# Differential attention: the pooling branch's GpSimd operations, each as two operations of half the columns

## The reference

```python
def diff_attention(q, k, v, lam, g_sub, lam_init):
    def one(qblk):
        s = jnp.einsum('bqhsd,bkhsd->bhsqk', qblk, k).astype(jnp.float32) * scale
        p = jax.nn.softmax(s, axis=-1)
        a = p[:, :, 0] - lam * p[:, :, 1]
        return jnp.einsum('bhqk,bkhe->bqhe', a.astype(v.dtype), v)
...
def multiscale_pool(u, w_pool, pool_scale):   # POOL_WINDOWS = (2, 4, 8, 16), one per 128 channels
...
    w = jnp.array(POOL_WINDOWS, dtype=jnp.int32)
    lo = jnp.clip(t - w // 2, 0, n)
    hi = jnp.clip(t + w - w // 2, 0, n)
    wsum = csum[:, hi, grp] - csum[:, lo, grp]
    pooled = (wsum / count - uf).astype(u.dtype)
    y = jnp.einsum('bngc,gcd->bngd', pooled, w_pool).reshape(b, n, BRANCH_WIDTH)
    return y * pool_scale
```

## Time and profile before

| what | value |
|---|---|
| median of 3 runs | 1798.11 us (1797.95 to 1799.56) |
| the profiled execution's own time | 1797.41 us |
| its span, first to last instruction | 1795.6 us |
| TensorE busy | 1742.4 us (97%) |
| VectorE busy | 1228.7 us (68%) |
| ScalarE busy | 805.7 us (45%) |
| GpSimd busy | 755.7 us (42%), 464 instructions |
| mean granted TensorE clock | 0.997 of full speed |

### The profile page before, as it was taken

The page is one execution under the profiler, slowest core; times in us unless marked ns, Lnnn a source line. Parts: engine busy times, 40 slices in busy tenths (PEclk is TensorE's granted clock), DMA queues, the critical chain, the costliest instruction groups (busy, mean ns, idle before and its releaser), DMA issues. The chain is left out here.

```text
span 1795.6 us, 25730 instructions
## 1 busy us (share of the span) xinstructions
PE 1742.4 (97%) x9180; PEld 1482.6 (83%) x9180; DVE 1228.7 (68%) x1719; ACT 805.7 (45%) x1580; POOL 755.7 (42%) x464
## 2 busy tenths in 40 slices
PE   8999999999998999999999999999999999999998
PEld 6997888888877899888888878778888888888886
DVE  3528688879948999677743366876556556476767
ACT  3435343434637788655530045733333333344453
POOL 0307678776534877520022241455555555400000
PEclk9999999999999999999999999999999999999999
DMA  8333233435777566412024332223323323386734
GB/s 312 118 101 125 111 117 153 162 132 188 258 194 181 137 164 180 115 32 71 1 103 154 131 141 95 94 94 105 117 93 105 130 103 106 126 273 203 257 107 176
DMA packets 98376, 249.86 MB, mean 139 GB/s; under 512 B 12258, under 2 KB 25954, under 8 KB 98147
## 3 DMA queue, kind: packets, MB, share of 16 engines
q1 hardware_dynamic: 98274, 248.52, 41.6%
HBM read 183.07 MB, written 65.41 MB: 138 GB/s over the span
## 5 line engine op out<-in xcount | busy, mean ns | idle before, releaser
L729 POOL TENSOR_TENSOR ring<-raw_w,ring 128x512 fp32r<-128x512 f32 x120 | 187.0, 1576 | 138.7 <-ACT ring L600 138.6
L78 PE MATMUL psum<-h_hi,ring 128*128 128x512 f32 x400 | 156.5, 391 | 2.6 <-ACT z L646 2.0
L79 PE MATMUL psum<-h_lo,ring 128*128 128x512 f32 x400 | 156.3, 391 | 0.0
L80 PE MATMUL psum<-h_hi,ring 128*128 128x512 f32 x400 | 156.1, 390 | 0.0
L78 PE MATMUL psum<-u_slot 128*128 128x512 f32 x308 | 120.4, 391 | 1.0 <-DVE u_slot L2898 0.9
L80 PE MATMUL psum<-u_slot 128*128 128x512 f32 x308 | 120.1, 390 | 0.0
L79 PE MATMUL psum<-u_slot 128*128 128x512 f32 x308 | 119.9, 389 | 0.0
L600 ACT ACTIVATE ring<-raw_w 128x512 fp32r<-128x512 f32 x120 | 72.6, 625 | 100.0 <-DVE raw_w L889 32.8
L1353 DVE TENSOR_REDUCE mx<-psum 128x1 f32<-128x1280 f32 x64 | 95.1, 1487 | 7.0 <-PE psum L1239 6.2
L1286 ACT ACTIVATE e<-psum,neg_m 128x1280 f32<-128x1280 f32 x64 | 85.0, 1329 | 31.6 <-DVE neg_m L1354 31.6
L2497 POOL TENSOR_TENSOR cut_lo<-i_raw,cut_hi 128x512 fp32r<-128x512 f32 x44 | 66.9, 1520 | 59.2 <-ACT cut_hi L2352 59.2
(11 more groups left out here) (409 smaller groups left out, 5222.2 us busy)
## 6 DMA issues: line engine op xcount, KB each, us to landing
raw_w<-in_w_pairs SPq DMA_DIRECT2D x40, 512.0 KB, 4.6
qk_dram<-room SPq DMA_DIRECT2D x26, 512.0 KB, 3.6
room<-in_w_ada SPq DMA_DIRECT2D x24, 512.0 KB, 5.3
gates_dram<-ost SPq DMA_DIRECT2D x24, 512.0 KB, 3.0
b_g<-gates_dram SPq DMA_DIRECT2D x8, 1536.0 KB, 7.5
stage<-in_w_ff SPq DMA_DIRECT2D x22, 512.0 KB, 5.9
i_raw<-in_w_ff SPq DMA_DIRECT2D x22, 512.0 KB, 4.8
f_dram<-h SPq DMA_DIRECT2D x22, 512.0 KB, 3.3
```

The source lines that it names most:

```text
L78: pe.matmul(out, sh, mh, start=first, stop=False, skip_group_check=onto)
L79: pe.matmul(out, sh, ml, start=False, stop=False, skip_group_check=onto)
L80: return pe.matmul(out, sl, mh, start=False, stop=last, skip_group_check=onto)
L729: pool.tensor_tensor(w_lo[i], source(p, i), w_hi[i].bitcast(F32), ALU.subtract).then_inc(w_lo_ready, 1)
```

## The change

Each of the 26 operations of the pooling is issued as two, over the first and the second half of its columns. `halves` issues the first half with `ch.did` (it counts, nothing waits) and the second with `ch.link` (GpSimd then waits for both). The halves of an addition over 1039 columns have 519 and 520. Loads, buffers, the order and the 16 pieces stay.

```diff
+            def halves(op, n=SEQ):
+                ch.did(op(slice(0, n // 2)))
+                ch.link(op(slice(n // 2, n)))
+
             for g, w in enumerate(POOL_WINDOWS):
                 pool.wait_ge(u_in, 32 * (g + 1))
                 src, width, step, i = upad, WW, 1, 0
                 while step < w:
                     dst = win[i]
-                    ch.link(pool.tensor_tensor(dst[:, 0:width - step], src[:, 0:width - step], src[:, step:width], ALU.add))
+                    halves(lambda c: pool.tensor_tensor(dst[:, c], src[:, c], src[:, c.start + step:c.stop + step], ALU.add), width - step)
                     src, width, step, i = dst, width - step, 2 * step, 1 - i
                 other = win[i]
-                ch.link(pool.tensor_tensor(other[:, 0:SEQ], src[:, PAD - w // 2:PAD - w // 2 + SEQ], inv[:], ALU.mult))
-                ch.link(pool.tensor_tensor(other[:, 0:SEQ], other[:, 0:SEQ], upad[:, PAD:PAD + SEQ], ALU.subtract))
+                off = PAD - w // 2
+                halves(lambda c: pool.tensor_tensor(other[:, c], src[:, off + c.start:off + c.stop], inv[:, c], ALU.mult))
+                halves(lambda c: pool.tensor_tensor(other[:, c], other[:, c], upad[:, PAD + c.start:PAD + c.stop], ALU.subtract))
                 pool.sem_inc(u_used, 1)
-                ch.link(pool.tensor_copy(pooled_hi[:, g, :], other[:, 0:SEQ]))
-                ch.link(pool.tensor_tensor(pooled_lo[:, g, :], other[:, 0:SEQ], pooled_hi[:, g, :].bitcast(F32), ALU.subtract))
+                halves(lambda c: pool.tensor_copy(pooled_hi[:, g, c], other[:, c]))
+                halves(lambda c: pool.tensor_tensor(pooled_lo[:, g, c], other[:, c], pooled_hi[:, g, c].bitcast(F32), ALU.subtract))
```

## The result

The changed kernel takes 1802.06 us (median of 11 runs, 1801.08 to 1804.13), the kernel before 1798.89 us (11 runs, 1796.28 to 1801.11). The ratio is 1.0017, 95% interval 1.0009 to 1.0025: about 3 us slower. The forecast was 1791.5 us, with a range to 1795.6. The profiled execution has a span of 1799.6 us against 1795.6.

The account below looks back on a forecast made before the run. TensorE, busy 97%, was taken as the bound: 7.8 us of waits less 1.2 left gain 6.6, with nothing for GpSimd's extra, so 1791.5 us against the median of 1798.11; range 1789.6 to 1795.6.

Parts of the forecast that it names:

- No queue, transfer or order is changed: In the pooling, 26 operations become 52, and nothing else in queues, transfers or order changes.
- its loads are issued on its own progress: In the sum: TensorE's loads follow TensorE's own progress, so the 6.6 us gain counts as reaching the end.
- What bounds the kernel, and what the waits cost: TensorE, 97% busy, loses 7.7 us waiting for VectorE's line 1368 beside the pooling; the first half microsecond is free.
- What VectorE waits for: Line 1368 gets in between unwaited halves; its longest wait falls from 2.2 to 1.1 us, leaving 1.2 us on TensorE's path.
- What GpSimd pays: Pooling: 0.14 us per added operation, 3.6 us in all; with collisions and idle time it ends 4.7 us later.
- The side estimate with 6.9 us for the starts: By the Trainium skill, 0.26 us per start, 6.9 us in place of 3.6; time about 1 us above the forecast.
- What hides that: The 16 pieces behind the pooling absorb GpSimd's lateness; the margin before line 1821 shrinks from 6.8 to 3.0 us.
- the four: Rivals: pieces late (chance 0.22), no hand-over between halves (0.06), GpSimd becomes the bound (0.05), gain lost behind the stage (0.05).
- The first: Rival: beyond 3.0 us extra on GpSimd the pieces come late and line 1821 waits; 1794.0 to 1796.7 us; chance 0.22.
- Rival 3: GpSimd becomes the bound outright if over 14.3 us later at the 16 pieces; 1805.8 us; chance 0.05.
- or shrink and return later: Sign of a wrong prediction: TensorE's waits shrink by less than 4 us, or shrink and come back later.
- The price of a wait: TensorE's wait for VectorE's line 1368 costs its length beyond the first, free half microsecond.

Follow-up runs that it names:

- e5: The changed kernel with q and k loads of heads 2, 3 and the window issued ahead of the waits for GpSimd: 1792.78 us, ratio 0.9964 to the kernel before.
- e10: e5 with GpSimd waiting behind the first half of each pair as well: 1792.32 us, ratio 0.9962 to the kernel before.
- e8: The kernel before, whole operations, with two loads of late sums (512 KB each) issued ahead of head 2's load: 1801.56 us, ratio 1.0019.
- e1: The changed kernel with head 2's six q and k loads issued ahead of the fourth pooling load: 1804.35 us, ratio 1.0028 to the kernel before.

## Why the prediction was wrong

The step that failed is the claim that GpSimd's progress moves no transfer that TensorE needs: "No queue, transfer or order is changed", and in the sum "its loads are issued on its own progress". Head 2's loads hang on GpSimd's `u_used`. They had 1.4 us of room and not the whole gain of 6.6, and the wait for them (8.25 us and 2.1 us of slow clock) took the gain back. By its own steps:

- *What bounds the kernel, and what the waits cost*: right. From 562 us on 8.2 us of waits for line 1368 became 1.9 (7.8 and 1.2 in the forecast), and with the loads out of the way the kernel gains 6.1 us (e5) where 6.6 were forecast. That the two gains agree so closely is in part luck: the interval of e5 reaches from 4 to 9 us, and its profiled execution still waits 3.9 us.
- *What VectorE waits for*: right. The longest line 1374 from 562 to 632 takes 2.64 us, which is 1.1 us of standing still, a half operation less 0.19 as forecast. The mean is 1.96 us where 1.8 was said, and the hand-over takes place between unwaited halves (the 2.53 us at 567.88, and e10).
- *What GpSimd pays*: the price of a split is right (two halves 2.06 us, one whole 1.92), and the odd start at column 519 costs nothing (1.05 us). That the pooling became 4.5 us longer where 4.7 were forecast is in part luck: its idle time ahead of windows 2 to 4 shrank by 2.5 us and not 0.8 (4.85 to 2.3), so the operations with their collisions took 7.0 us more and not 5.5. The side estimate with 6.9 us for the starts doesn't follow from its own margin: 6.9 - 3.6 - 3.0 is 0.3 us, not about 1.
- *"No queue, transfer or order is changed"*: true of the code and the step that failed. I followed GpSimd's lateness along its own list, to the pieces and their first reader, and not along SyncE's. SyncE waits for `u_used` with head 2's seven loads queued behind the wait, so GpSimd's progress sets their issue. The SyncE rows of the kernel before show it: head 2's first load is issued 0.84 us behind the upad load that waits for GpSimd.
- *"Its loads are issued on its own progress"* (in the sum): wrong for heads 2 and 3. This sentence carried the whole gain to the end. Had I put the landing (631.4) beside the first use (632.8), the margin of 1.4 us would have capped the gain made ahead of head 2, before any delay. e8 measures that margin by spending it.
- *What hides that*: the 11.2 us ahead of piece 6 were called semaphore clearing that stays. In e5 this idle time is 1.07 us:

```profile
674.78 1.90 POOL L1230 TENSOR_TENSOR late_w<-late_w,silu_x 128x1024 f32<-128x1024 f32 x1 [1.07 <-issue]
```

  So the clearing takes no more than that. In the kernel before piece 6's load was issued behind head 3's, at 655.69, and took 20.4 us from issue to landing: 676.1, one microsecond ahead of piece 6's start at 677.11. So GpSimd stood for that load, though the row names "issue". Idle time in front of a load gives way when GpSimd itself is late (in e1, where the pooling takes 74.3 us, 9.6 us of it are left), so the room at the pieces is larger than the 3.0 us that I gave it. In the changed kernel it was 6.9 us, with TensorE late as well; in e5, where the piece's load is issued earlier, 8.5 (734.4 to 742.88).
- *Rivals*: none of the four was what happened. The first had the right form (a reader waits because GpSimd is late and TensorE early) and the wrong place. Rival 3, on the slower side, needed 14 us of lateness; here the third `u_used` came 1.6 us later in the span, 3.4 us later counted from the start of the pooling, and that was enough. Of the forecast's own signs, "or shrink and return later" is the one that came.
- *The price of a wait* was taken as its length. Behind 8.25 us of idle time 2.1 us of slow clock came on top.

## What to carry to other kernels

An engine that gets faster needs its loads earlier: put the landing of every load that it will meet beside its first use, also where no wait shows, since a load that lands 1.4 us ahead leaves no trace in the waits and caps the gain. Follow a delayed engine into every queue that waits on its semaphores, and look at what is queued behind that wait. Where VectorE and GpSimd exclude each other, halving GpSimd's operations takes most of the waits away for 0.14 us an operation; do it together with moving the loads that wait on GpSimd. All these figures are of this kernel.

## What the runs showed that I had not expected

Seven loads of one head (4.2 MB by the sizes of the rows: two of 512 KB, five of 640 KB) take some 22 us to land when they are queued together, with the two pooling loads ahead of them and two of 512 KB behind, though a single 512 KB load of the pieces lands in 3 to 4 us. TensorE's clock fell to 0.50 during a wait of 8.25 us and stayed below full for some 4.5 us of work behind it; in e8 the 128x512 products took 0.63 us behind a wait of 3.44 us too; during the waits of up to 1.6 us between 564 and 632 us in the kernel before it stayed at 1.00. GpSimd operations of 519 and 520 columns cost the same 1.05 us, whether they start at an even or an odd column.
